# Routing three token tiles inside the last output tile, and picking the first expert's rows by 0/1 products

## The reference

```python
h = rms_norm(x, norm_mix)
proj = h @ w_in                     # queries, keys, values, S5 input u, gates
merged = gated sum of three branches (neighbourhood attention, S5, cross attention)
x = x + merged @ w_out              # "output tiles": 4 tiles of 128 tokens
h2 = rms_norm(x, norm_ffn)
coarse = h2 @ w_coarse + b_coarse   # 4 groups
fine = h2 @ w_fine + b_fine         # 16 experts, 4 in each group
group = argmax(coarse); top 2 experts of that group; weights by softmax
for e in range(16):                 # each expert on the tokens that chose it
    a = silu(h2[rows] @ w_gate[e]) * (h2[rows] @ w_up[e]) * weight
    x[rows] += a @ w_down[e]
return rms_norm(x, final_norm)
```

## Time and profile before

| | |
|---|---|
| time, median of 3 runs | 642.37 us (641.95 to 643.02) |
| the profiled execution's own time | 641.48 us |
| its span, first to last instruction | 639.9 us |
| mean granted clock of PE | 0.971 |
| PE busy | 584.6 us (91%) |
| DVE busy | 421.8 us (66%) |
| ACT busy | 322.4 us (50%) |
| POOL busy | 240.5 us (38%) |

### The profile page before, as it was taken

The page is one execution under the profiler, slowest core; times in us unless marked ns, Lnnn a source line. Parts: engine busy times, 40 slices in busy tenths (PEclk is TensorE's granted clock), DMA queues, the critical chain, the costliest instruction groups (busy, mean ns, idle before and its releaser), DMA issues.

```text
span 639.9 us, 9019 instructions
## 1 busy us (share of the span) xinstructions
PE 584.6 (91%) x3149; PEld 472.9 (74%) x3149; DVE 421.8 (66%) x768; ACT 322.4 (50%) x531; POOL 240.5 (38%) x235
## 2 busy tenths in 40 slices
PE   2998998999999999999999999996599999999960
PEld 2687887889877777777777888886477878888850
DVE  4988513795386573554743378425788999999936
ACT  4867332222345424453343336215279988998732
POOL 3417996993000900000000000023744766776810
PEclk9999999999999999999999999997699999999995
DMA  9993327220262222122312337963699999999264
GB/s 305 201 203 102 102 64 188 76 68 1 68 188 75 67 67 79 57 64 69 96 67 66 99 99 175 350 237 132 204 360 393 382 393 393 386 401 347 53 136 158
DMA packets 89233, 111.47 MB, mean 174 GB/s; under 512 B 19647, under 2 KB 66913, under 8 KB 89192
## 3 DMA queue, kind: packets, MB, share of 16 engines
q1 hardware_dynamic: 76952, 93.13, 44.1%
q0 software_dynamic: 7280, 15.12, 9.1%
q10 hardware_dynamic: 4960, 2.70, 1.7%
HBM read 102.08 MB, written 14.75 MB: 183 GB/s over the span
## 4 chain that ended last, share of the span: by engine, by line
PE 58%; DMA 21%; DVE 9%; issue 4%; POOL 3%; ACT 2%; SPq 1%; ACTq 0%; DVEq 0%; POOLq 0%
DMA acc_scratch<-ysb,idx 17%; PE bank L1529 15%; PE bank L1531 15%; PE bank L1530 15%; PE bank L1710 2%; PE bank L1684 2%; PE bank L1697 2%; DMA xg<-h_scratch,idx 2%; DVE w_lo L966 2%; DVE h_lo L991 1%; PE bank L1815 1%; POOL tok_scratch L2157 1%; PE bank L1645 1%; DMA xf<-acc_scratch 1%; PE bank L1649 1%
## 5 line engine op out<-in xcount | busy, mean ns | idle before, releaser
L966 DVE TENSOR_TENSOR w_lo<-raw,w_hi 128x1024 fp32r<-128x1024 f32 x55 | 74.6, 1356 | 104.9 <-ACT w_hi L560 104.4
L1529 PE MATMUL bank<-h_hi,w_hi 128*128 128x512 f32 x320 | 128.8, 402 | 2.3 <-DVE w_lo L966 1.7
L1531 PE MATMUL bank<-h_hi,w_lo 128*128 128x512 f32 x320 | 125.0, 390 | 0.0
L1530 PE MATMUL bank<-h_lo,w_hi 128*128 128x512 f32 x320 | 124.6, 389 | 0.0
L1416 DVE TENSOR_TENSOR e_lo<-eraw,e_hi 128x2048 fp32r<-128x2048 f32 x48 | 108.6, 2289 | 6.9 <-ACT e_hi L807 6.9
L807 ACT CAST e_hi<-eraw 128x2048 fp32r<-128x2048 f32 x48 | 91.9, 1917 | 8.1 <-PE bank L1531 8.1
L560 ACT CAST w_hi<-raw 128x1024 fp32r<-128x1024 f32 x55 | 57.5, 1045 | 33.7 <-PE bank L1531 33.7
L2107 POOL TENSOR_TENSOR wcf<-wcf,prt 128x160 f32<-128x160 f32 x1 | 0.5, 457 | 195.8 <-DMA wcf<-in_moe_w_fine 195.8
L1529 PEld LDWEIGHTS bank<-h_hi,w_hi 128*128 128x128 f32 x320 | 60.1, 188 | 16.4 <-DVE w_lo L966 2.4
L1531 PEld LDWEIGHTS bank<-h_hi,w_lo 128*128 128x128 f32 x320 | 60.1, 188 | 13.1
L1530 PEld LDWEIGHTS bank<-h_lo,w_hi 128*128 128x128 f32 x320 | 60.2, 188 | 11.2
(11 more groups left out here) (388 smaller groups left out, 1233.2 us busy)
## 6 DMA issues: line engine op xcount, KB each, us to landing
raw<-in_w_in SPq DMA_DIRECT2D x40, 512.0 KB, 3.9
eraw<-in_moe_w_gate SPq DMA_DIRECT2D x32, 512.0 KB, 10.7
eraw<-in_moe_w_up SPq DMA_DIRECT2D x32, 512.0 KB, 13.7
eraw<-in_moe_w_down SPq DMA_DIRECT2D x32, 512.0 KB, 14.0
raw<-in_w_out SPq DMA_DIRECT2D x8, 512.0 KB, 3.8
x_sb<-in_x SPq DMA_DIRECT2D x4, 512.0 KB, 4.6
raw<-in_w_mem_kv SPq DMA_DIRECT2D x4, 512.0 KB, 6.3
raw<-in_w_br_na SPq DMA_DIRECT2D x4, 512.0 KB, 3.3
```

Source lines behind the costliest of these rows:

```text
L966: dve.tensor_tensor(v(l_, o, [1, 1024]), v(raw, 1024 * (c % RAW), [1, 1024]), raw32(v(h_, o, [1, 1024])), SUB).then_inc(sem("w_lo_done"), 1)
L1529: pe.matmul(dst, w[0], x[0], start=first, stop=False)
L1530: pe.matmul(dst, w[0], x[1], start=False, stop=False)
L1531: return pe.matmul(dst, w[1], x[0], start=False, stop=last)
```

## The change

1. `inverse_root` takes the root without DVE's mean first, and replaces two Newton steps by one step in another form (reciprocal, multiply-add, reciprocal).
2. `forward_b` moves one chunk later (c = 6 and 7).
3. The eight loads of u go from ACT's queue at c = 12 to SP's queue behind the load of chunk 14.
4. Inside output tile 3 PE turns x of tile 2, computes the logits of tiles 0 to 2 (`logit_parts`, `logit_sums`: four groups of 32 columns side by side, then a sum of the four), turns the first half of tile 3 (its first bank is closed at half of the tile), and counts places for three tiles; DVE routes three tiles meanwhile. Tile 3 is routed behind it alone.
5. The rows of expert 0 are no longer gathered from memory. PE multiplies h2 (in SBUF) by 0/1 matrices `hotf` (`first_tokens`, 32 products of 128 by 128 by 128 in plain fp32), which gives them already turned.
6. DVE's e_lo of unit 0 comes in two halves before the routing of tile 3; e_lo of unit 1, one `hot` and `slot_list(2)` now stand in front of the weights of the tokens (`wts`); `slot_list(3)` moves into PE's first step. POOL gathers for experts 1 and 2, then goes on as before.
7. SP loads units 5 and 6 earlier (unit 6 in another place of SBUF).
8. At the end DVE normalises tile n - 1 right after the sum of tile n.

```diff
         def roots(k, j, n):
-            act.wait_ge(sem("means"), k)
-            act.activation(v(stat, 16 + j, [1, n]), v(stat, 8 + j, [1, n]), ACT.Sqrt).then_inc(sem("roots"), 1)
+            act.wait_ge(sem("squares"), sums_of(k))
+            act.activation(v(stat, 16 + j, [1, n]), v(stat, j, [1, n]), ACT.Sqrt, scale=0.25 / D,
+                           bias=v(stat, 57 if k == NT + 3 else 49, [1, 1])).then_inc(sem("roots"), 1)
...
-            if c in (5, 6):
+            if c in (6, 7):
                 dve.wait_ge(sem("ct_ready"), 2)
-                forward_b(c - 5)
+                forward_b(c - 6)
...
         for c in range(5, NCH):
             load(c)
+            if c == 14:
+                sp.wait_ge(sem("u_out"), 16)
+                sp.wait_ge(sem("bias_ready"), 4)
+                for t in range(T5):
+                    sp.dma_start(v(upk, 0, [K5, G5], [1, K5], p0=16 * t, pn=16),
...
+        sp.wait_ge(sem("last_out"), 2)
+        load_unit(0, 2, 5)
         sp.wait_ge(sem("out_k"), NT)
-        load_unit(0, 2, 5)
+        load_unit(1, 2, 6)
         sp.wait_ge(sem("h2_out"), 16 * (NT + 2))
-        sp.wait_ge(sem("logits"), NT)
+        sp.wait_ge(sem("logits"), 3)
+        sp.wait_ge(sem("xt"), 2)
         sp.wait_ge(sem("xg1"), 16)
-        load_unit(1, 2, 6)
         load_unit(2, 1, 7)
...
+        def logit_parts():
+            pe.wait_ge(sem("wcf_g"), 1)
+            pe.wait_ge(sem("x2_took"), 2 * (NT - 1))
+            for k in range(KD):
+                ins = pe.matmul(pv(0, 0, [1, 3 * P], p0=32 * (k % 4), pn=32), v(wcf, 32 * k, [1, 32]),
+                                v(x2T, SEQ * k, [1, 3 * P]), start=k < 4, stop=k >= 4)
+            ins.then_inc(sem("logits"), 1)
...
+        def first_tokens(n, j):
+            if n == 0:
+                pe.matmul(pv(4 + j, 0, [1, 512]), v(onesb, 0, [1, P]), v(upper, 0, [0, 512]), start=True, stop=False)
+                pe.wait_ge(sem("hotf"), 1)
+            if n == NT - 1:
+                pe.wait_ge(sem("hotf"), 2)
+                pe.wait_ge(sem("h2_scaled"), 1)
+            for k in range(4):
+                ins = pe.matmul(pv(4 + j, P * k, [1, P]), v(h2, D * n + 4 * j + k, [KD, P]), v(hotf, P * n, [1, P]),
+                                start=False, stop=n == NT - 1 and k == 3)
+            if n == NT - 1:
+                ins.then_inc(sem("xt"), 1)
...
+        for c in range(C_OUT, NCH):
+            out_part(NT - 1, c, False)
+            if c == C_OUT:
+                for j in range(2):
+                    x2_turn(2, j)
+            if c == C_OUT + 2:
+                logit_parts()
+            if c == C_OUT + 3:
+                logit_sums()
+            if c == C_OUT + 5:
+                x2_turn(NT - 1, 0)
+            if c == C_OUT + 6:
+                last_logits(0)
+                places(True)
+        first_tokens(0, 0)
+        x2_turn(NT - 1, 1)
+        first_tokens(0, 1)
+        last_logits(1)
+        first_tokens(1, 0)
+        first_tokens(1, 1)
+        first_tokens(2, 0)
+        places(False)
+        first_tokens(2, 1)
+        slot_list(1)
+        first_tokens(NT - 1, 0)
+        first_tokens(NT - 1, 1)
+        slot_list(2)
+        counts()
...
         (DVE, behind the norms of tiles 0 to 2)
+        dve.wait_ge(sem("last_out"), 1)
+        x2_add(NT - 1, 0).then_inc(sem("x2_half"), 1)
+        dve.wait_ge(sem("logits"), 2)
+        route(0, NT - 1)
+        dve.wait_ge(sem("iotas"), 1)
+        place(0, NT - 1)
+        dve.wait_ge(sem("e_hi_done"), 1)
+        first_lo(0)
+        dve.wait_ge(sem("out_k"), NT)
+        x2_add(NT - 1, 1).then_inc(sem("x2"), 1)
+        first_lo(1).then_inc(sem("e_lo_done"), 1)
+        one_hot(1, 0, NT - 1)
+        inverse_root(NT + 3, NT - 1, 1)
+        dve.wait_ge(sem("logits"), 3)
+        route(NT - 1, 1)
+        place(NT - 1, 1)
+        one_hot(1, NT - 1, 1).then_inc(sem("hot"), 1)
+        one_hot(2, 0, NT).then_inc(sem("hot"), 1)
+        slot_list(1)
+        xt_rest(0, 0)
+        unit_lo(1, 1, 1)
+        one_hot(3, 0, NT).then_inc(sem("hot"), 1)
+        slot_list(2)
         (then route_arg, rows, slot_list(3), flag and wts as before)
...
         (POOL)
         pool.wait_ge(sem("h2_out"), 16 * (NT + 2))
-        for e in range(3):
-            pool.wait_ge(sem("idx0"), e + 1)
+        for e in range(1, 3):
+            pool.wait_ge(sem("idx0"), e)
             gather(e)
         store_x2(NT - 1)
         pool.wait_ge(sem("rows"), 1)
...
-        pool.wait_ge(sem("idx0"), NHOT)
-        pool.wait_ge(sem("xt"), 2)
+        pool.wait_ge(sem("idx0"), NHOT - 1)
         gather(3)
...
         (DVE, end)
+        last_sum(0)
+        for n in range(1, NT):
+            last_sum(n)
+            last_norm(n - 1)
+        last_norm(NT - 1)
```

More of the change, by code:

```diff
@@ L426, in build @@
     H2_BANK = (4, 7)
+    LOGIT_BANK = (1, 1, 1, 0)
     B_BANK = (4, 5, 7, 3)
@@ new lines, in counts @@
+        def counts():
+            for n in range(NT):
+                ins = pe.matmul(pv(6, 64, [1, 16]), v(onesb, 0, [1, P]), v(selb, 16 * n, [1, 16]),
+                                start=n == 0, stop=n == NT - 1)
+            ins.then_inc(sem("places"), 1)
+        def first_tokens(n, j):
[10 more added lines that the diff above has]
+                ins.then_inc(sem("xt"), 1)
@@ L1819, in _, with slot_list @@
+        def slot_list(e):
+            pe.wait_ge(sem("hot"), e)
+            for n in range(NT):
+                ins = pe.matmul(pv(HOT_BANK[e], 0, [1, 2]), v(hot, P * (NT * e + n), [1, P]), v(tokf, 2 * n, [1, 2]),
+                                start=n == 0, stop=n == NT - 1)
+            ins.then_inc(sem("hot_used"), 1)
         for c in range(C_OUT, C_OUT + 4):
@@ L1873, in gate_up @@
                 kk = 4 * half + k
+                if kk == 7 and within:
+                    slot_list(3)
+                    tokens(*within)
                 ins = split(pv(1 if odd else 0, 0, [1, 512]), [v(x[odd], P * kk, [1, P]) for x in (xt_hi, xt_lo)],
@@ L1898, in step @@
                 ins.then_inc(sem("at"), 1)
-            if not peeled or e < 15:
-                tokens(e + 1, (e0 + 1) % 3, 16 * (2 * i + (e0 + 1) // 3 + 1))
-            if not peeled or e < 16:
-                gate_up(e, 1 if first else 3 * e, 1, 1 if first else 0, odd)
+            slot = (e0 + 1) % 3
+            after = (e + 1, slot, 16 * (2 * i + (e0 + 1) // 3 + (1 if slot else 0)))
+            if not first and (not peeled or e < 15):
+                tokens(*after)
+            if first:
+                pe.wait_ge(sem("xt_lo"), 2)
+                gate_up(0, 1, 1, 1, odd, after)
+            elif not peeled or e < 16:
+                gate_up(e, 3 * e, 1, 0, odd)
             if not first:
@@ L2136, in _ @@
         pool.tensor_copy(v(rt, 1040, [1, NE]), v(eidx, 0, [1, NE])).then_inc(sem("iotas"), 1)
+        for half in range(2):
+            pool.wait_ge(sem("x2" if half else "x2_half"), NT if half else 1)
+            o = 512 * half
+            pool.tensor_tensor(v(h2, D * n + o, [1, 512]), v(x_sb, D * n + o, [1, 512]), v(gffb, o, [1, 512]),
+                               MUL).then_inc(sem("h2_g"), 1)
         pool.wait_ge(sem("h2_scaled"), 1)
```

376 lines of the change are left out of this document (197 added, 179 removed).

## The result

| | before | changed |
|---|---|---|
| median | 642.16 us (4 runs, 641.48 to 643.02) | 655.69 us (4 runs, 650.46 to 659.50) |
| ratio, 95% interval | | 1.0197 (1.0157 to 1.0238): slower, by 1.6 to 2.4% |
| profiled execution, its own time | 641.48 us | 659.28 us |
| its span | 639.9 us | 657.7 us |

I had forecast 643.9, which is +1.5 us, with 637.5 to 648 over all cases. The side was right; the time is 11.8 us above the forecast and outside the range.

The account below looks back on a forecast made before the run. PE waits for the router, then sets the expert stage's pace; POOL's scatter path ends within about 1 us of PE's. Terms -0.9 + 2.2 - 1.9 + 3.4 - 1.6, plus 0.3 for clock, gave +1.5: 643.9 us, range 637.5 to 648.

Parts of the forecast that it names:

- First norm: Start, mean to scaling of the second pair: five small DVE operations instead of eight, nothing covers them, -0.9 us.
- B: Chunk 8: both forward_b calls now stand before v_take(0), so PE's turn comes at 72.1 instead of 69.82, +2.2 us.
- u: PE's wait for the landing of u goes, as SP issues its loads 30 us earlier, -1.9 us.
- end: Last output tiles: norm n - 1 behind sum n lets DVE run through, -1.6 us.
- Inside tile 3: Router work put into output tile 3: 4.9 us added to 11.0 of PE, so the tile ends at 436.8.
- To the first product: Router to first expert product: eight groups of first_tokens take 7.6 us, first product at 447.9, 8.9 us earlier.
- The scatters: POOL's eight scatters begin at 455.9, six are held by e_lo, the last ends at 474.7 (before 467.91).
- What follows: After the scatters: PE waits 10 us for expert 3's rows, wcur at 486.0, expert 0's down product +3.4 us.
- From there PE's pace and the chain of adds are as before: Expert stage behind expert 0's down product: pace unchanged, so the +3.4 us goes to the end whole.
- POOL's chain no later: Rival, scatters: e_lo do not hold them, 636.2 us; chance 0.33 for all below -0.2%.
- the two cancel: Rival, expert start: lists +2 late, landings short in quiet queues, 641.1 to 643.6 us; chance 0.22.
- PE's clock: Rival, first_tokens: clock falls, 4 us more until wts, 647 to 648 us; chance 0.1, inside the 0.45 for slower.

Follow-up runs that it names:

- f3: Kernel before with only B moved (forward_b before the low parts of chunks 7 and 8, not 6 and 7): 647.92 us, 1.0083 of before.
- e4: Kernel before with only the new norms, u loaded by SP and last norms interleaved with the sums: 637.41 us, 0.9932 of before.
- e2: Changed kernel with h2 laid out so that the weights of first_tokens lie side by side: 645.79 us, 1.0002 of the kernel before.
- e5: e2 with forward_b back at its place in the kernel before: 644.88 us, 0.9917 of the kernel before.
- a_again: Changed kernel run once more, unedited, on another occasion: 650.72 us, 1.0104 of the kernel before.
- g1: Changed kernel with each e_lo of the expert stage cut into two operations of 1024 columns: 641.26 us, 0.9992 of the kernel before.
- f2: e6 with each e_lo of the expert stage cut into two operations of 1024 columns: 629.41 us, 0.9794 of the kernel before.
- e6: e5 with expert 3's gather ahead of the scatters, and remaining slot lists, rows and wts made earlier: 631.44 us, 0.9811 of the kernel before.

## Why the prediction was wrong in size

Point by point, by its own steps.

- **First norm, -0.9: the saving is there, its worth is open.** Ahead of the second pair DVE waits for a transfer, in both kernels. From that wait's end to the scaling it takes 2.1 us before and 1.1 in the changed kernel, which is the 1.0 counted. But the transfer landed 0.76 later, so that the first product is 0.26 earlier:

```profile
11.63 0.22 DVE L980 COPY prm<-stat 16x128 f32<-16x128 f32 x1 [1.48 <-DMA stat<-in_s_log_dt]
```

```profile
12.39 0.22 DVE L1009 COPY prm<-stat 16x128 f32<-16x128 f32 x1 [3.13 <-DMA stat<-in_s_log_dt]
```

  In the eleven profiles with the new norm the first product begins at 18.93 to 20.64, in the three with the old one at 19.99 to 20.36. I had not put this transfer into the path.
- **B, +2.2: the wait right, the price too low.** `vm` is waited for 3.9 us, the turn begins at 71.98 (predicted 72.1). Missed was the lower clock behind the wait. By f3 the term is +5.3 (3.4 to 7.3). I had added 0.3 for the clock in another place and nothing here.
- **u, -1.9, and end, -1.6: right as far as shown.** e4 gives -4.4 with the norm, all three together. From the first product to the first turn of x2 its profile is 2.1 us shorter than the one before, and PE's wait for u is gone; at the end, from the start of the last sum to the end of the last norm, 5.1 us pass in the changed kernel (649.50 to 654.59) against 9.8, and part of that is given back ahead of it, where sums now wait behind norms.
- **Inside tile 3** (11.0 and 4.9 from 420.6 are 436.5, not 436.8): `logit_parts` takes 1.50 us (1.4 predicted) and the sums 0.74 (0.7): right.
- **To the first product: the step that failed first.** "The eight groups take 7.6" was sized from a row with weights side by side. They take 15.9, since the weights lie 32 bytes apart (333 ns a load against 194). Row list of expert 1 at 451.8 instead of 446.0, `wts` 463.2 instead of 455.6, scatters from 464.03 instead of 455.9. e2 shows that it is the layout; e5, with weights side by side and B back, has its first scatter at 455.73.
- **The scatters, six held, 18.8 us: four held, 15.3.** The rule (0.9 behind the end of the e_lo) was right, its phase not. The prediction also took the held scatters as speaking against the inference of the Trainium skill, page "SBUF — State Buffer", on descriptor generation; as said above, they leave it open, since only the beginning of an issue is held. The last scatter ended 11.4 later than before where I had 6.8.
- **What follows, `ysb` +3.4: the first add came 11.2 later.** The chain from scatters over lists to `wcur` was 12.9 us (11.3 counted). PE's wait for expert 3's rows was 7.5 us, where I had 10.
- **"From there PE's pace and the chain of adds are as before": the second step that failed.** I had applied the hold to scatters and gathers and not to the adds, whose chain leaves only 0.6 us an expert (9.3 - 8.7). In the changed kernel's first profile the stage lost 9.7 us, 4.6 of them held time; in a_again, of the lower group, it lost nothing. With halves (g1) the upper group does not come.

In the profiled execution the forecast of about +3 us up to the first add met +11.2, the stage of +0 met +9.7, and the end of -1.6 met -3.1.

The rivals: POOL's chain no later, and the two cancel, did not come about; PE's clock stayed 1.00 in `first_tokens`, so the price that I gave that rival (647 to 648) would have come closer for a wrong reason.

What stays open: why the kernel before, whose profile has a stage of 104 us, had two executions near 650 in some 80, while kernels with the changed router and the long e_lo had one to six long ones in 4 to 12. That its adds find a steady phase (2.01 to 2.34 us from the seventh to the twelfth, each 9.1 to 9.5 behind the last) is seen in its profile, not tested. From the end of an issue to the next add pass up to 3 us more than 7.1 in the long stages, 5.1 us in sum in the changed kernel; no run separates that from the holds, and g1 has such rounds with hardly any hold.

## What to carry to other kernels

Price a matmul by a row whose weights have the same spacing, not only the same shape: here 32 bytes apart cost 333 ns a load against 192. Where POOL issues indirect transfers in a chain, look for long DVE operations on SBUF beside it: cutting a 2.28 us operation in two cost DVE 0.07 us and gave 1.1 to 2.0% on the changed kernel (g1), of which some 0.6% came behind the stage, and nothing clear of noise where the chain was early (f2 against e6). When a wait is moved on TensorE's path, add what follows it to its price: here 5.3 us in all (3.4 to 7.3), of which 2.1 are more waiting (3.9 less 1.8); the rest goes with the stretch at the lower clock.

## What the runs showed of the hardware

- An indirect transfer's issue on POOL that begins 0.06 us or more into a DVE subtraction with both operands in SBUF (128x2048, 2.28 us) ends a fixed time behind that operation's end (scatter 0.84 to 0.92, gather 0.92 to 1.00, add 1.46 to 1.56), with no exception in 221 cases, and passes between two operations that stand back to back. One that is already running when the subtraction begins is not held (at most 0.08 us in 78 cases).
- A one-operand multiplication of 128x2048 in SBUF (1.23 us) holds such an issue also when it begins 0.5 to 1.0 us into it: thirteen ended 0.08 to 0.12 us behind it.
- In a plain fp32 product a weight load of 128 columns took 333 ns with its elements 32 bytes apart, 307 at 64 bytes, 192 to 194 side by side.
- One program took times in two groups some 10 us apart (647.88 to 652.11 and 659.28 to 661.38); with the long operation cut in halves eleven of twelve executions lay within 5.6 us.
